# Value products of a decoder layer's attention heads: ordered by key block over both branches instead of one branch after the other

## The reference, cut to what matters

```python
# stick breaking, for each block of 128 queries
weights = jnp.where(strict, jnp.exp(log_beta + suffix), 0.0)
outs.append(jnp.einsum('bhqk,bhkd->bhqd', weights.astype(vb.dtype), vb))
# forgetting attention
p = jax.nn.softmax(jnp.where(causal, z, -jnp.inf), axis=-1)
outs.append(jnp.einsum('bhqk,bhkd->bhqd', p.astype(vb.dtype), vb))
# around them
y_sb = merge_heads(o_sb) @ w_proj_sb;  y_fx = merge_heads(o_fx) @ w_proj_fox
merged = sigmoid(g_sb) * y_sb + sigmoid(g_fx) * y_fx
x = layer_norm(ALPHA * x + merged @ w_out);  x = layer_norm(ALPHA * x + conv_glu(x))
```

## Time and profile before

| what | value |
|---|---|
| median of 3 runs | 756.1 us (756.01 to 756.1) |
| the profiled execution: its own time | 755.87 us |
| the profiled execution: span of its instructions | 754.1 us |
| PE busy | 743.7 us (99%) |
| PE weight loads busy | 620.6 us (82%) |
| DVE, ACT, POOL busy | 365.3, 318.1, 338.7 us |
| granted TensorE clock, mean | 0.997 |
| attention stage (halves 0 to 7) | about 83 to 296 us of the span |

### The profile page before, as it was taken

One profiled execution on the slowest core, in us unless ns is written; L12 is line 12 of the kernel. 1 busy time (PEld: TensorE's weight loads), 2 busy tenths in 40 slices (PEclk: granted clock), 3 DMA queues, 4 the chain that ended last, 5 costly groups with the idle time before them and its releaser, 6 DMA issues.

```text
span 754.1 us, 9599 instructions
## 1 busy us (share of the span) xinstructions
PE 743.7 (99%) x3528; PEld 620.6 (82%) x3528; DVE 365.3 (48%) x506; ACT 318.1 (42%) x429; POOL 338.7 (45%) x245
## 2 busy tenths in 40 slices
PE   9999999999999999999999999999999999999996
PEld 6888788888888888888898888888888888888884
DVE  3339679879789764446552112211221122322567
ACT  4322584774765775662123332323332243423410
POOL 6654254434533424992005445454544453655800
PEclk9999999999999999999999999999999999999998
DMA  8223413314214123761003322222232327332002
GB/s 311 96 98 113 125 37 114 102 56 116 81 56 139 57 84 112 279 223 56 1 1 113 107 88 98 97 91 103 86 109 83 111 83 280 111 110 85 29 29 83
DMA packets 24477, 78.33 MB, mean 104 GB/s; under 512 B 2944, under 2 KB 3328, under 8 KB 24448
## 3 DMA queue, kind: packets, MB, share of 16 engines
q1 hardware_dynamic: 24448, 77.94, 30.8%
HBM read 71.63 MB, written 2.10 MB: 98 GB/s over the span
## 4 chain that ended last, share of the span: by engine, by line
PE 93%; DVE 3%; ACT 1%; issue 1%; DMA 1%; SPq 0%; DVEq 0%; ACTq 0%
PE ps L978 90%; PE ps L1076 2%; DVE sb_t L800 1%; DMA w_raw<-w_stream_in 0%; PE ps L1156 0%; DVE fx_nmax L792 0%; DMA fx_k<-k_bias_rows 0%; ACT fx_p L555 0%; DVE sb_k L757 0%; DVE qk_lo L693 0%; DVE fx_lo L693 0%; DVE sb_t L823 0%; SPq L342 0%; DVE fx_k L693 0%; ACT sb_t L549 0%
## 5 line engine op out<-in xcount | busy, mean ns | idle before, releaser
L414 POOL TENSOR_TENSOR w_lo<-w_raw,w_hi 128x512 fp32r<-128x512 f32 x220 | 295.9, 1368 | 374.0 <-ACT w_hi L476 368.4
L476 ACT ACTIVATE w_hi<-w_raw 128x1024 fp32r<-128x1024 f32 x109 | 115.4, 1060 | 218.6 <-DMA w_raw<-w_stream_in 218.5
L978 PE MATMUL ps<-x1T_hi,w_hi 128*128 128x512 f32 (+1 forms) x376 | 141.3, 376 | 0.0
L978 PE MATMUL ps<-x1T_lo,w_hi 128*128 128x512 f32 (+1 forms) x376 | 141.2, 375 | 0.0
L978 PE MATMUL ps<-x1T_hi,w_lo 128*128 128x512 f32 (+1 forms) x376 | 141.2, 375 | 0.0
L941 DVE SCALAR_TENSOR_TENSOR conv<-ps,col,conv 128x511 f32<-128x511 f32 (+1 forms) x44 | 33.0, 749 | 166.8 <-ACT conv L656 162.5
L978 PE MATMUL ps<-xT_hi,w_hi 128*128 128x512 f32 x264 | 105.9, 401 | 1.2 <-ACT g_all L524 1.2
L978 PE MATMUL ps<-xT_hi,w_lo 128*128 128x512 f32 x264 | 103.2, 391 | 0.0
L978 PE MATMUL ps<-xT_lo,w_hi 128*128 128x512 f32 x264 | 102.9, 390 | 0.0
L978 PEld LDWEIGHTS ps<-x1T_lo,w_hi 128*128 128x128 f32 x376 | 70.8, 188 | 12.9
L978 PEld LDWEIGHTS ps<-x1T_hi,w_hi 128*128 128x128 f32 x376 | 70.8, 188 | 12.9
(11 more groups left out here) (142 smaller groups left out, 1131.9 us busy)
## 6 DMA issues: line engine op xcount, KB each, us to landing
w_raw<-w_stream_in SPq DMA_DIRECT2D x109, 512.0 KB, 3.3
wout_raw<-w_out_in SPq DMA_DIRECT2D x8, 512.0 KB, 5.0
r_raw<-w_stream_in SPq DMA_DIRECT2D x5, 512.0 KB, 10.7
xT_raw<-xT_in SPq DMA_DIRECT2D x8, 256.0 KB, 6.5
x<-x_tok_in SPq DMA_DIRECT2D x4, 512.0 KB, 4.2
ln_rows<-rows_in SPq DMA_DIRECT2D x4, 512.0 KB, 5.7
out_dram<-x SPq DMA_DIRECT2D x8, 256.0 KB, 2.0
sb_q<-sb_q SPq DMA_DIRECT2D x8, 128.0 KB, 2.3
```

The lines of the kernel that those rows point to most:

```text
L414: lo = nc.gpsimd.tensor_tensor(w_lo[:, slot, cs], w_raw[:, slot, cs], plain(w_hi[:, slot, cs]), ALU.subtract)
L476: nc.scalar.activation(w_hi[:, slot, :], w_raw[:, slot, :], ACT.Copy).then_inc(hi_ready, 1)
L978: return nc.tensor.matmul(out_, lhs, rhs, start=start, stop=stop, skip_group_check=True)
```

## The change

The loops over the two branches and over the key blocks are exchanged. The 16 matmuls of a half, their operands, widths and output banks stay the same.

```diff
                 pe.wait_ge(v_split, pair * 2 + 2)
-                for b, split, hi, lo, mixed in ((1, fx_w_split, fx_hi, fx_lo, fx_mixed),
-                                                (0, sb_w_split, sb_hi, sb_lo, sb_mixed)):
-                    place = 512 * MIXED_BANKS[h][b]
-                    pe.wait_ge(split, h + 1)
-                    pe.wait_ge(block_read, read_before + placed - 1 + (1 - b))
-                    for r in range(SB):
+                weights = ((1, fx_hi, fx_lo, fx_mixed), (0, sb_hi, sb_lo, sb_mixed))
+                for r in range(SB):
+                    for b, hi, lo, mixed in weights:
+                        place = 512 * MIXED_BANKS[h][b]
+                        if r == 0:
+                            pe.wait_ge(fx_w_split if b else sb_w_split, h + 1)
+                            pe.wait_ge(block_read, read_before + placed - 1 + (1 - b))
                         v = v_parts[:, b, r, e, :, :].rearrange("p t d -> p (t d)")
                         for part in (hi, lo):
                             last = product(ps[:, place + P * r:place + 512], v,
                                            part[:, KEY_OFF[r]:KEY_OFF[r] + P * (SB - r)],
                                            start=r == 0 and part is hi, stop=r == SB - 1 and part is lo)
-                    last.then_inc(mixed, 1)
+                        if r == SB - 1:
+                            last.then_inc(mixed, 1)
```

## The result

The changed kernel takes 761.77 us in the median of 6 runs (760.9 to 763.1), beside 756.0 us for the kernel before on the same chip. The ratio is 1.0075, with a 95% interval of 1.0064 to 1.0085: slower by 0.75%. A later comparison of the same two kernels (5 runs and 9) gave 761.65 against 756.37, ratio 1.0068 (1.0054 to 1.0082). The profiled execution took 760.90 us against 755.87, its span 759.1 us against 754.1. The 5.0 us between these two profiles are what the rest explains; the medians lie 5.3 to 5.8 apart.

The account below looks back on a forecast made before the run. PE, busy for 99% of the span, was taken as the bound. 7 x 0.66 + 0.79 - 0.30 = 5.11 us on the profiled 755.87 gave 760.98, so a median of 761.2; range 760.0 to 762.8.

Parts of the forecast that it names:

- The work of PE does not change: Value products of each half: same 16 products and weight loads, so exchanging the loops changes their sum by 0.
- Rival (b): Value products: alternating between two PSUM banks costs 0.05 per change, 2.4 us in all, giving 763.6; chance 0.05.
- The wait that moves: sb's first product waits uncovered for ACT's read of the last fill: 0.66 us lost per half, 0.79 in half 0.
- Rival (a): Ahead of sb's first product: the last fill's read hides after all, time stays 756.1; chance 0.05.
- Rival (d): sb's first weight load is pulled ahead during the wait, 0.9 us less in all, giving 760.3; chance 0.05.
- What is queued behind: After the waiting product: later fx_o_low delays fx_o_sum, DVE's row and sb_t, but all stay hidden, adding no time.
- Rival (c): One half later: fx_o_sum or DVE's row come late, seven halves lose 0.2 each, giving 762.6; chance 0.07.
- What the loss gives back: Start of half 2: PE arrives 0.66 us later, so its wait for the fx_k transfer vanishes, -0.30 us.
- The sum: Whole kernel: losses less the time given back make 5.11 us, so 760.98 profiled and a median of 761.2.

Follow-up runs that it names:

- e1: The kernel before with its product order kept, but the waits for sb moved up behind the second product; 760.86 us against 756.34, ratio 1.0061.
- e2: The changed kernel's wait behind two products, but ordered fx block 0, sb blocks 0 to 3, fx blocks 1 to 3; 760.94 us, ratio 1.0062 to the kernel before.
- e8: The changed kernel with the two waits ahead of sb's first product exchanged, fill read first; 761.11 us, ratio 1.0064 to the kernel before.
- e9: The changed kernel run once more without edits; 761.65 us against 756.37 for the kernel before.
- e4: The changed kernel's interleaving, but sb starts only behind six products (three fx key blocks); 756.99 us, ratio 1.0012 to the kernel before.
- e6: The kernel before, with ACT reading half 0's first fill before waiting for the maxima; 756.67 us, ratio 1.0009.
- e10: The changed kernel with sb's waits one product further up, behind the first fx product; 763.01 us in one run.
- e5: The kernel before, with SP issuing the stacking transfers of fx's q ahead of its wait for k; 757.76 us, ratio 1.0020.

## Why the prediction was right, by its own steps

**The work of PE does not change: shown.** The same wait with three different orders (changed, e1, e2) gives 3.138, 3.146 and 3.139 us. The narrow products step by 0.11 at the end of a half (158.77, 158.88, 158.99). Rival (b) would have put the changed kernel 0.3 above e1 in each half; it lies 0.008 below it.

**The wait that moves: right in size.** 0.66 was worked out and 0.661 measured in seven halves; 0.79 for half 0 and 0.788 measured, with `sb_lo` as the later condition there and only there. The price of a release with two waits, 0.11 and then the load, was taken from a far row and held; e8 turned it into the other bound (0.05) by exchanging the waits, so both ends were real. Rival (a), that the read hides, is refuted by the timeline of half 2. Rival (d), by the rule of the Trainium skill ("TensorE: Matmul & The Clock Gate", Part 2) that a weight load can be pulled ahead of matmuls in flight, did not come about. The rows agree with the rule where a load has no wait: the one for the second fx product starts at 155.85, with the first product. The load of sb's first product carries a wait of its own and started at 156.85, behind the release, though PE had been idle.

**What is queued behind: hidden, as forecast.** `fx_o_low` starts at f + 3.12 (forecast 3.10). The followers of half 2 in the changed kernel, to compare with the earlier trace rows:

```profile
159.60 0.68 DVE L844 TENSOR_TENSOR fx_o_sum<-ps,fx_o_low 64x512 f32<-64x512 f32 x1 [3.54 <-ACT fx_o_low L585]
...
162.92 1.67 DVE L693 TENSOR_TENSOR oT_lo<-sb_o_sum,oT_hi 64x512 fp32r<-64x512 f32 x1
165.19 1.09 DVE L792 TENSOR_REDUCE fx_nmax<-ps 128x1 f32<-128x128 f32 x3 [0.60 <-PE ps L978]
...
161.02 1.24 ACT L544 ACTIVATE sb_t<-ps 128x1280 f32<-128x1280 f32 x1
```

`fx_o_sum` ends at f + 4.43 and the first fill isn't held. DVE keeps 0.60 us of idle time where 0.1 was expected: its row from `fx_o_sum` to `oT_lo` took 4.99 us, not 5.54, one of the casts being shorter (0.81 instead of 1.34). `sb_t` starts at f + 5.17, 0.04 later than due. Rival (c) did not occur.

**What the loss gives back: right mechanism, wrong size.** The term of -0.30 measured -0.53. It took the idle time of the row for the loss. But rows overlap: the matmul ahead is drawn for 0.39 us where it holds PE for 0.23, and the one behind starts its row 0.08 before it can go on, as its own length of 0.47 instead of 0.39 shows. So 0.16 + 0.08 = 0.24 us are lost beside the shown 0.30. The same holds for the new waits: shown 0.42, lost 0.66. The prediction used this for what the new waits would show and not for the term taken back. The transfer doesn't land at a fixed time either. In the kernel before one of its four issues took 1.39 us instead of 0.60, and it landed 7.36 us behind half 1's first value product; in the first profile of the changed kernel no issue was long and it landed at 6.64. So that profile alone doesn't show that the 0.66 us were enough. e9 does: there an issue took 1.32 us, the transfer landed at 7.30, and PE, which came to these scores at 7.71, had no wait. The long issue in the kernel before, and then in e9:

```profile
132.78 1.39 SPq L342 DMA_DIRECT2D fx_k<-k_bias_rows  x1
```

```profile
134.59 1.32 SPq L342 DMA_DIRECT2D fx_k<-k_bias_rows  x1
```

**The sum and the median.** The sum gave 5.11 and the profiles differ by 5.03; with the right -0.53 it would have been 4.88, and the late start of this execution (0.12) covered half of the error of 0.23. That part of the agreement is luck. The forecast of 761.2 lies 0.6 under the measured median of 761.77. The losses in the attention stage don't vary, but the waits in the first 10 us do, by 0.9 us between the two profiles of the changed kernel, and the kernel before spread over 754.9 to 758.0 in the 16 runs beside e1 to e4. Why three of the first six runs of the changed kernel lay at 762.4 or more is not settled, as those runs have no profile: e9 speaks for the start, but the six runs of the kernel before beside them spread over 0.8 us only (755.3 to 756.1).

**Two readings to set right.** The granted clock was not at the upper level in all slices: the last digit of PEclk is 8 in both kernels, and in the last 4.1 us of the kernel before, where PE has no work, it was 0.50; no term hangs on it. And the 1.2 us of half 0, named as a place where another engine could give time back, are slack for the one engine that was tried: with ACT's read 6 us earlier nothing was gained (e6).

## What to carry to other kernels

Before moving a wait forward in a queue that is the bound, read what stands ahead of it now as its cover, and compare it with the end of the work waited for, each from the same fixed point; the loss is the difference plus the release and the load. An order that is neutral in work is not neutral if one of its pieces needs a bank that was just filled. Idle time on an engine with overlapping rows understates a loss, and an idle time that a profile shows (the 1.2 us of half 0) is not a gain to be had before the next condition in line has been looked at.

## What the runs showed of the hardware

Two conditions on one product have a price that depends on their order. With the one that ends later on the weight load, the load started 0.05 us behind the release (half 0 of the changed kernel, the other seven halves of e8); with that one on an instruction of its own ahead of the load, 0.11 (the other way round).

The granted clock was 1.00 over the attention stage (83 to 300 us) of the changed kernel and of e10, in which each half has a new wait of PE that costs 0.66 to 1.03 us.

Four transfers of 128 KB share the queue with a load of 512 KB. With the two of q issued 1.85 us earlier in the half (e5), the first of them landed 0.4 us later than before (5.65, 5.09 and 5.31 us behind the first value product of halves 1, 3 and 5, beside 5.20, 4.70 and 4.92), and the load 1.0, 1.9 and 1.1 us later. The reason stays open.
